# Probability copies in two parts in every attention stream, and a reordered stream with features beside its last iterations

## The reference, cut to what matters

```
p = hx @ w_in                       # x: 512 rows, context: 256 rows, the same weights
oa = window_gqa_latent(qa, ka, va, cka, cva, sink)      # 8 heads, one softmax each, width 64
logits = [einsum('bqhmd,bkhmd->bmhqk', q, k) * scale]   # 4 heads, two maps each
outs = [einsum('bhqk,bkhd->bqhd', p[:, 0] - lam * p[:, 1], v)]   # width 128
ob = rmsnorm_2(o, subln_g) * (1 - lam_init)             # each head of ob, over its 128 values
yx = concatenate([oa, ob]) @ w_out                      # 1024 features in, 1024 out
```

## Time and profile before

| | |
|---|---|
| median of 3 executions | 4091.64 us (4091.26 to 4095.93) |
| the profiled execution | 4095.51 us, its span 4093.6 us |
| busy share of the span | PE 93%, PEld 78%, DVE 51%, ACT 31%, POOL 29% |
| mean granted clock of TensorE | 0.963 |
| its_ab's stream, then its features | 335.9 us, then 26.3 us |

### The profile page before, as it was taken

The page is one execution under the profiler, slowest core; times in us unless marked ns, Lnnn a source line. Parts: engine busy times, 40 slices in busy tenths (PEclk is TensorE's granted clock), DMA queues, the critical chain, the costliest instruction groups (busy, mean ns, idle before and its releaser), DMA issues. The chain is left out here.

```text
span 4093.6 us, 48762 instructions
## 1 busy us (share of the span) xinstructions
PE 3811.3 (93%) x19370; PEld 3197.6 (78%) x19370; DVE 2074.7 (51%) x3437; ACT 1268.6 (31%) x1971; POOL 1202.9 (29%) x548
## 2 busy tenths in 40 slices
PE   6999988999999999899989897899999889999998
PEld 4777866888777787688867776799999778877886
DVE  5446745565654674565555655533333665533113
ACT  3332234222333223422234443311111245533222
POOL 1233433444322343344421011122222110023442
PEclk9899999999999999999999998999999899999999
DMA  3123422333212342233321001133333100012332
GB/s 91 53 69 112 135 78 63 107 103 112 80 54 69 112 135 78 73 104 102 112 68 37 22 27 34 59 93 107 95 108 99 56 18 16 27 47 77 93 97 73
DMA packets 544400, 316.70 MB, mean 77 GB/s; under 512 B 35828, under 2 KB 517167, under 8 KB 544175
## 3 DMA queue, kind: packets, MB, share of 16 engines
q1 hardware_dynamic: 526495, 278.97, 23.5%
q10 hardware_dynamic: 17680, 34.61, 2.6%
HBM read 311.44 MB, written 2.10 MB: 77 GB/s over the span
## 5 line engine op out<-in xcount | busy, mean ns | idle before, releaser
L451 POOL TENSOR_TENSOR wlo<-wraw,whi 128x1024 fp32r<-128x1024 f32 (+6 forms) x544 | 1202.7, 2216 | 2855.2 <-ACT whi L444 2855.1
L467 PE MATMUL acc<-hh,whi 128*128 128x512 f32 (+2 forms) x2744 | 1066.1, 389 | 30.7 <-DVE hl L624 23.2
L468 PE MATMUL acc<-hl,whi 128*128 128x512 f32 (+2 forms) x2744 | 1035.9, 378 | 0.0
L469 PE MATMUL acc<-hh,wlo 128*128 128x512 f32 (+2 forms) x2744 | 1035.3, 377 | 0.0
L444 ACT ACTIVATE whi<-wraw 128x1024 fp32r<-128x1024 f32 (+6 forms) x544 | 522.9, 963 | 652.1 <-DMA wraw<-in_w_up 185.1
L467 PEld LDWEIGHTS acc<-hh,whi 128*128 128x128 f32 x2744 | 522.8, 191 | 146.5 <-issue 30.9
L468 PEld LDWEIGHTS acc<-hl,whi 128*128 128x128 f32 x2744 | 522.8, 191 | 91.9 <-issue 12.7
L469 PEld LDWEIGHTS acc<-hh,wlo 128*128 128x128 f32 x2744 | 521.8, 190 | 83.8
L1516 DVE TENSOR_TENSOR t<-acc,sq 128x768 f32<-128x768 f32 (+1 forms) x44 | 36.3, 825 | 448.1 <-PE acc L469 448.1
L467 PE MATMUL ob<-hh,whi 128*128 128x512 f32 (+3 forms) x576 | 214.6, 373 | 6.5 <-DVEq L814 6.0
L467 PE MATMUL acc<-act1h,whi 128*128 128x512 f32 x528 | 209.4, 397 | 1.4 <-DVE act1l L1524 1.4
(11 more groups left out here) (383 smaller groups left out, 6215.3 us busy)
## 6 DMA issues: line engine op xcount, KB each, us to landing
wraw<-in_ffn_w SPq DMA_DIRECT2D x120, 512.0 KB, 3.9
wraw<-in_w_in SPq DMA_DIRECT2D x102, 512.0 KB, 3.9
wraw<-in_w_up SPq DMA_DIRECT2D x88, 512.0 KB, 3.8
ada_w<-in_ada_w ACTq DMA_DIRECT2D x64, 512.0 KB, 4.1
ada_w<-in_ada_w SPq DMA_DIRECT2D x32, 512.0 KB, 4.2
wraw<-in_w_down SPq DMA_DIRECT2D x32, 512.0 KB, 4.0
wraw<-in_w_out SPq DMA_DIRECT2D x16, 512.0 KB, 4.0
wraw<-in_w_mkv SPq DMA_DIRECT2D x16, 512.0 KB, 3.9
```

The lines of the kernel that those rows point to most:

```text
L451: e.tensor_tensor(wlo[0:rows, s, a:b, 0:w], wraw[0:rows, s, a:b, 0:w], whi[0:rows, s, a:b, 0:w].bitcast(F32), ALU.subtract).then_inc(lo_re ...
L467: e.matmul(o, wh, xh, start=first, stop=False)
L468: e.matmul(o, wh, xl, start=False, stop=False)
L469: return e.matmul(o, wl, xh, start=False, stop=last)
```

## The change

It has three parts. First, in all streams the copy of the transposed probabilities is made in two instructions, the first three blocks (384 columns) and the rest; L926's first matmul waits for the first, its fourth for the second. Where there are at most 384 columns it stays one instruction. Second, in `its_ab` each group has its two-map iterations first and its local ones after. The prologue before the stream makes the two-map keys, queries and values of group 0 (`tile_kd`) and no longer the local ones, whose projections become the first jobs; `vd2` goes, the ticks are laid out anew, and the order of the slabs follows. Third, six of the eight features become twelve "feat" jobs of 384 columns beside the last twelve iterations (group 3's local ones). The roots and norms go into hooks after the steps 60 to 64. The features 1 and 3 are still made at the end, and the first slab of the output product takes k in the order 0, 2, 4, 5, 6, 7, 1, 3.

```diff
-        vd2 = z("vd2", [P, 6, P])
...
+        KF = [(k, k, P) for k in (0, 2, 4, 5, 6, 7, 1, 3)]
...
+        COPIED_FIRST = 3
...
-                    e.wait_ge(s_copied, c.at(s_copied, n))
+                    e.wait_ge(s_copied, c.at(s_copied, 2 * n - 1))
                     e.wait_ge(ob_free[0], c.next(ob_free[0]))
                     copied(False)
                     slot["pv"] = n
                     for j, vj in enumerate(t["v"]):
+                        if j == COPIED_FIRST:
+                            e.wait_ge(s_copied, c.at(s_copied, 2 * n))
                         mm = e.matmul(ob[0][:, 0:t["dv"]], sq[:, 0, j * P:j * P + P], vj, start=j == 0,
                                       stop=j == len(t["v"]) - 1)
...
-                    e.activation(sq[:, 0, 0:w], ptf[:, 0:w], ACT.Copy).then_inc(s_copied, 1)
+                    m = min(w, COPIED_FIRST * P)
+                    e.activation(sq[:, 0, 0:m], ptf[:, 0:m], ACT.Copy).then_inc(s_copied, 1 if m < w else 2)
+                    if m < w:
+                        e.activation(sq[:, 0, m:w], ptf[:, m:w], ACT.Copy).then_inc(s_copied, 1)
...
+        LAST_FEATURES = (1, 3)
...
-            load(sp, c, [(0, P, rows_of(ab, 0, 0, KT, 1024))])
-            queries(0)
-            load(sp, c, [(0, P, rows_of(ab, 0, 0, KT, 1152))])
+            for col in (1280, 512, 1792):
+                load(sp, c, [(0, P, rows_of(ab, 0, 0, KT, col))])
...
-                for col in (512, 1280) + ((1792,) if t == 0 else ()):
-                    load(e, c, [(0, P, rows_of(ab, 0, 0, KT, t * P + col))])
-                if t < 3:
-                    load(e, c, [(0, P, rows_of(ab, 0, 0, KT, t * P + P + 1792))])
-                    queries(t + 1)
-            turns(sp, c, 4, heads_ab)
+                for col in (512, 1280, 1792):
+                    load(e, c, [(0, P, rows_of(ab, 0, 0, KT, t * P + P + col))])
+                queries(t + 1)
+            load(sp, c, [(0, P, rows_of(ab, 0, 0, KT, 1024))])
+            queries(0)
+            load(sp, c, [(0, P, rows_of(ab, 0, 0, KT, 1152))])
+            turns(sp, c, 3, heads_ab)
...
-        def tile_kg():
-            tiles = [rope_ab(kgh, kgl), rope_ab(qgh, qgl), values_2(vg, kts=K8)]
+        def tile_kd():
+            tiles = [rope_ab(kdh, kdl), rope_ab(qdh, qdl), values_2(vd, kts=K8)]
...
+            def feat(f, after, t=None):
+                return [dict(kind="feat", T=384, span=P, src=ot2[:, 3 * i:3 * i + 3, f * P:f * P + P], hi=hh[:, f, 384 * i:384 * i + 384],
+                             lo=hl[:, f, 384 * i:384 * i + 384], after=after, normed=t) for i in range(2)]
+            out_ = rope_ab(kgh, kgl) + rope_ab(qgh, qgl) + values_halves(vg)
+            for t in range(3):
+                out_ += rope_ab(qdh, qdl) + rope_ab(kdh, kdl) + values_halves(vd) + rope_ab(qgh, qgl)
+            out_ += feat(0, 36) + feat(2, 36)
             for t in range(4):
-                out_ += rope_ab(qdh, qdl) + rope_ab(kdh, kdl) + (values_halves(vd) if t == 0 else [])
-                if t < 3:
-                    out_ += values_halves((vd2, vd)[t % 2]) + rope_ab(qgh, qgl)
+                out_ += feat(4 + t, 18 * t + 6, t)
             return out_
 
         def ticks_ab():
 
-            ticks, j = [None], 0
-            for t in range(4):
-                for span, tiles in ((10, 3 if t == 0 else 2), (8, 2 if t < 3 else 0)):
-                    n = min(span, 6) if span == 8 else span
-                    for i in range(tiles):
-                        m = n * (i + 1) // tiles - n * i // tiles
-                        long = (m + 1) // 2 if i == (2 if span == 10 else 0) else (2 * m + 1) // 3
-                        ticks += over(j, KT, long) + over(j + 1, KT, m - long)
-                        j += 2
-                    ticks += [None] * (span - (n if tiles else 0))
-            return ticks
+            ticks, j = over(0, KT, 2) + over(1, KT, 1) + over(2, KT, 1) + over(3, KT, 1) + over(4, KT, 1) + over(5, KT, 1), 6
+            for t in range(3):
+                for i, n in enumerate((3, 1, 3, 1, 2, 2, 3, 1)):
+                    ticks += over(j + i, KT, n)
+                ticks += [None, None]
+                j += 8
+            return ticks + [(j + i, 0, 0, True) for i in range(12)]
+
+        def normed_ab(e, c, t):
+
+            if t == 0:
+                e.wait_ge(subn_ready, 1)
+            for r in range(6):
+                o = ot2[:, r, (4 + t) * P:(5 + t) * P]
+                e.scalar_tensor_tensor(out=o, in0=o, scalar=hss[:, t * 6 + r:t * 6 + r + 1], in1=subg[:, :],
+                                       op0=ALU.mult, op1=ALU.mult).then_inc(heads_normed, 1)
...
-                            dv=HD, dst=ot2[:, r, t * HD + h * 256:t * HD + h * 256 + HD], s=(h,), need=(0, 10, 18, 26)[t], pair=True)
+                            dv=HD, dst=ot2[:, r, t * HD + h * 256:t * HD + h * 256 + HD], s=(h,), need=4 if t == 0 else 6 + 8 * t, need_v=6 + 8 * t, pair=True)
...
-                            ss=hss[:, t * 6 + r:t * 6 + r + 1], need=(6, 14, 22, 30)[t])
+                            ss=hss[:, t * 6 + r:t * 6 + r + 1], need=2 + 8 * t if t else 0, need_v=4 + 8 * t if t else 0)
             its = []
             for t in range(4):
-                its += [local(t, h, r) for r in range(6) for h in range(2)] + [diff(t, r) for r in range(6)]
+                its += [diff(t, r) for r in range(6)] + [local(t, h, r) for r in range(6) for h in range(2)]
             return its
...
-            pe_features(pe, c, ot2, KT, 6, normed=4)
-            pe_linear_y(pe, c, TC, hh, hl, KT, feat_ready, ada=(1, 3, 5, 7))
+            pe_features(pe, c, ot2, LAST_FEATURES, 6)
+            pe.wait_ge(s_ready, c.next(s_ready, c.here["made"] - c.at(s_ready, 0)))
+            pe_linear_y(pe, c, TC, hh, hl, KT, feat_ready, features=True, ada=(1, 3, 5, 7))
...
+            def heads_rooted():
+                act.wait_ge(ss_ready, 1)
+                act.activation(hss[:, :], hss[:, :], ACT.Ln, bias=small[:, 63:64], scale=1.0 / P).then_inc(act_step, 1)
+                act.wait_ge(act_step, c.next(act_step))
+                act.activation(hss[:, :], hss[:, :], ACT.Exp, scale=-0.5).then_inc(subn_ready, 1)
+            act_flow(act, c, its_ab(), jobs_ab(), ticks_ab(), hooks={60: heads_rooted})
+
+            act_features(act, c, hh, LAST_FEATURES, 6)
             act_linear_y(act, c, T=TC, y=y2, ada=(1, 3, 5, 7))
...
+            at_end = {60: lambda: dve.sem_inc(ss_ready, 1), 61: lambda: normed_ab(dve, c, 0), 62: lambda: normed_ab(dve, c, 1),
+                      63: lambda: normed_ab(dve, c, 2), 64: lambda: normed_ab(dve, c, 3)}
+            dve_flow(dve, c, its_ab(), jobs_ab(), ticks_ab(), hooks=at_end)
+            dve_features(dve, c, hh, hl, LAST_FEATURES, 6)
```

More of the change, by code:

```diff
@@ L469, in mm3, with slab @@
             return e.matmul(o, wl, xh, start=False, stop=last)
-        def slab(e, c, T, xh, xl, kts, M=P, fresh=0, free=True, c0=0, w0=0, ready=h_ready):
+        def slab(e, c, T, xh, xl, kts, M=P, fresh=0, free=True, c0=0, w0=0, ready=h_ready, late=range(KT)):
             w, s = weights(e, c), c.turn("slab")
@@ L477, in slab @@
             for j, (k, xk, rows) in enumerate(kts):
-                if fresh:
+                if fresh and xk in late:
                     e.wait_ge(ready, c.next(ready, fresh, view="slab"))
@@ L630, in dve_prenorm, with pe_linear_y @@
             dve_apply(e, c, xres, hh, hl, range(KT), segs)
-        def pe_linear_y(e, c, T, xh, xl, kt, ready, ada=(), flush=None):
-            kts = [(k, k, P) for k in range(kt)]
+        def pe_linear_y(e, c, T, xh, xl, kt, ready, ada=(), flush=None, features=False):
+            kts = KF if features else [(k, k, P) for k in range(kt)]
             def body(e, i):
                 for j in range(2):
-                    slab(e, c, T, xh, xl, kts, fresh=1 if ready and i + j == 0 else 0, ready=ready)
+                    slab(e, c, T, xh, xl, kts, fresh=1 if ready and i + j == 0 else 0, ready=ready,
+                         late=LAST_FEATURES if features else range(kt))
                     if 2 * i + j in ada:
@@ L814, in jrelease, with pe_flow @@
             e.sem_inc(proj_free if s is None else acc_free[s], 1)
-        def pe_flow(e, c, its, jobs, ticks, xh, xl, wide=False, extra=None, early=()):
+        def pe_flow(e, c, its, jobs, ticks, xh, xl, wide=False, extra=None, early=(), hooks={}):
             c0 = c.here.get("made", 0)
@@ L889, in part @@
                     e.wait_ge(ob_free[0], c.at(ob_free[0], 1 + t["after"] - slot.get("pv", 0)))
-                    for r in range(4):
+                    if t.get("normed") is not None:
+                        e.wait_ge(heads_normed, 6 * t["normed"] + 6)
+                    for r in range(t["src"].shape[1]):
                         mm = e.transpose(jbank(s)[:, r * P:r * P + P], t["src"][:, r, :], ident[:, :])
@@ L955, in pe_flow, with act_flow @@
                     extra[1]()
+                if n in hooks:
```

(13 more changed lines are left out.)

62 lines of the change are left out of this document (26 added, 36 removed).

## The result

The changed kernel takes 4046.6 us (median of 4, 4043.08 to 4054.06) against 4091.75: a ratio on record of 0.988, 95% interval 0.9867 to 0.9894 (the medians alone give 0.989). The profiled execution took 4054.06 us (span 4052.3), so between the two traces lie 41.3 us of span.

A forecast was written before the change was run, and what follows sets the result against it. TensorE, busy 93% of the span, was taken as the bound, leaving its idle and half-clock time to win. Split copy -8.7, its_ab +9.8 and features' end -20.8 made -19.7 us: 4091.6 to 4072 us, range 4053 to 4086.

The forecast's parts named there:

- the waits: PE's waits for the probabilities' copy, first block and its_c: 28 places shortened by 0.31 us each, 8.7 us gained.
- ACT's extra instructions: Two copies for one cost ACT 0.18 us more in 144 iterations; claimed to be hidden behind PE.
- The tail: Last twelve iterations of its_ab with features beside them: about 47.2 us, as ACT and DVE are tied in each step.
- the end: From its_ab's last value product to the output product: 5.5 us instead of 26.3, a gain of 20.8.
- the middle stretches: Three its_ab stretches, group t's local with group t+1's two-map iterations: PE idle 7.2 us each, 21.6 in all.
- The start: Beginning of its_ab: PE idle 4.5 us, 2.4 as before and about 1 us twice at a rope's DVE instructions.
- the 2 us that I had added to the tail for half clock: Half clock likely in its_ab's last part, adding only 2 us because DVE and ACT set the step.
- Rival (b): The features hide in its_ab's last twelve steps, about 2.8 us a step, 13 us less: 4059 us, chance 0.20.
- I count six among 13 heads and leave them in the sum: its_c: six clock falls among 13 heads, 1.6 us each, assumed to remain after the change.
- rival (c): its_c's waits shrink from 0.84 to 0.53 us and its clock falls go, 6 x 1.6 us: 4062 us, chance 0.08.
- my ledger: Sum of PE's work, idle time and half-clock cost for its_ab, with the other gains leading to 4072 us.
- Rival (e): Half clock puts PE into the chain in its_ab's last twelve steps, 2.7 us more each: +32, 4104 us, chance 0.07.

The follow-up runs named there:

- fill_c: Kernel before, copy whole, with six useless transposes ahead of PE's copy wait at one its_c iteration in four, other waits in old order: 4083.1 us, ratio 0.9969.
- feat_late: Changed kernel, but DVE subtracts a feature one step later, behind the next maxima: 4048.8 us, ratio 0.9886.
- first_5: Changed kernel with five blocks (640 columns) in the first copy instead of three: 4067.3 us, ratio 0.9924.
- wait_both: Changed kernel, copy in two instructions, but the value product's first matmul waits for both: 4077.9 us, ratio 0.9959.
- fill_before: Kernel before with the same its_c transposes, but the ob_free wait put ahead of the s_copied wait in all other iterations too: 4092.2 us, ratio 0.9997.

## Why the prediction was wrong

**Right: the waits.** Forecast 8.7 us, measured 1.8 + 1.6 + 4.9 = 8.3; 0.53 us for 13 of the 16 in its_c, none ahead of the fourth block, ACT's extra instructions hidden.

**Right: its_ab and the features.** The tail 47.3 against 47.2 us, the end 5.7 against 5.5, the end's gain 20.6 against 20.8. In the middle stretches PE was idle 83.07 - 74.80 = 8.3, 7.9 and 6.8 us against 7.2 each. The start had 1.7 where I took 4.5. Ahead of the tail PE was busy 269.5 us (forecast 270.4) and idle 24.7 (26.1), and the 2 us that I had added to the tail for half clock didn't come: with these the stream was 4.2 us shorter than forecast. Rival (b), features that hide, is out. In the tail I had PE idle for 23.6 us; it stood for 10.4, since at a clock of 0.71 the same work takes longer, and as I had argued that cost little.

**Wrong: the clock.** The step that failed is "I count six among 13 heads and leave them in the sum". I had seen that each fall follows a wait of 0.84 us, and set the chance that shorter waits remove them at 0.08, because seven equal waits had no fall. That argument is false: it shows that such a wait doesn't always bring a fall, not that falls come without it. What it should have called for is a rate at each length of the wait: 3 to 7 heads of twelve at 0.74 to 0.90 us and 0 at 0.52, as the runs show. Filling the wait instead of shortening it removes the falls too (fill_c). And rival (c) stopped at its_c: the earlier trace rows held the waits of its_1, but I never asked for the clock of those streams, 0.87 and 0.89 in the second of each layer. Both together are the 21 us that are missing, about 11 in its_c and 10 in its_1: my ledger's 4072 less 21 is 4051, within 5 us of the measured. Rival (c), at 6 x 1.6 us, had nearly the size of its_c's part and nothing for its_1, so its 4062 was still too high. That the falls of its_1's second streams go with its shorter waits is shown by count (0 of 10 against 9 of 12); no run filled the waits there with the copy left whole, as fill_c does in its_c.

**The rule on the page.** The Trainium skill (TensorE: Matmul & The Clock Gate, section "Why this matters for your kernels") lets the full clock last unless PE idles for several microseconds between bursts. The runs disagree: with waits of 0.74 to 0.90 us 3 to 7 heads of twelve had a fall, with 0.52 none. I had quoted the contradiction and drawn nothing from it for the sum.

**Rival (e)** didn't happen in the changed kernel. In feat_late PE came into the chain and the tail grew by 5.3 us, not by the 32 of the rival; what of it half clock cost was not tested.

## What to carry to other kernels

Before a wait of PE is shortened, ask for the granted clock of every stretch behind such waits, and price the wait as its own length plus its share of the falls: here 8.3 us of waits brought 29. A wait that can't be shortened can be filled with useless transposes, if no other wait moves for it. Work laid beside iterations is priced by the tie that it makes between engines (here 12 us for 20.7 gained), and undoing one tie helps only if the bank behind it is free as well.

## What the runs showed of the hardware

Waits of 0.74 us are enough for the granted clock to fall to 0.5 behind some of them (1.6 us for each head of its_c that has a fall); whether one comes differs from head to head with equal instructions and from execution to execution, and a longer wait is no sure sign of one: in its_1's second streams waits of 1.26, 0.79 and 0.79 us had a fall twice (first_5), waits of 1.42, 0.96 and 0.96 us none (wait_both). Behind 0.52 us no head of its_c had one, in seven traces. The filling's effect on the whole was that of its_c's falls alone only where no other wait changed (fill_c 4083.1, fill_before 4092.2 us); why the swapped order of two waits costs the rest is open. Where VectorE and ScalarE set the step, the tail of its_ab took 46.5 us at a clock of 1.00 and 47.8 at 0.79.
